# The modulation product with w_ada as the stationary operand

## The reference, cut to what matters

```python
def _adaln(cond, w, b):
    return jax.nn.silu(cond) @ w + b        # w: (1024, 6144), b: (6144,)
mod_ctx = _adaln(c_ctx[None], w_ada[l], b_ada[l])
mod_lat = _adaln(c, w_ada[l], b_ada[l])
...
shift1, scale1, gate1, shift2, scale2, gate2 = jnp.split(mod[:, None, :], N_MOD, axis=-1)
m, s_fin = _mixer(x * (1 + scale1) + shift1, lp, s0)
x = _layer_norm(DEEPNORM_ALPHA * x + gate1 * m, ...)
f = ffn(x * (1 + scale2) + shift2)
x = _layer_norm(DEEPNORM_ALPHA * x + gate2 * f, ...)
```

## Time and profile before

| | us |
|---|---|
| median of 3 runs | 2322.9 (2321.09 to 2323.04) |
| profiled execution, its time | 2311.55 |
| profiled execution, span of its core | 2309.8 |
| TensorE products busy | 2015.3 (87%) |
| TensorE loads of the stationary operand busy | 1704.7 (74%) |
| VectorE busy | 1136.7 (49%) |
| ScalarE busy | 757.7 (33%) |
| mean granted TensorE clock | 0.917 of 2.4 GHz |

### The profile page before, as it was taken

How to read it: one execution, slowest core, us unless ns; L and a number is a source line. 1 busy time by engine, 2 the same in 40 slices (tenths; PEclk the granted TensorE clock), 3 DMA queues, 4 the chain that set the end, 5 groups by cost and what they waited for, 6 DMA issues and landing times.

```text
span 2309.8 us, 30916 instructions
## 1 busy us (share of the span) xinstructions
PE 2015.3 (87%) x13189; PEld 1704.7 (74%) x13189; DVE 1136.7 (49%) x1458; ACT 757.7 (33%) x918; POOL 106.6 (5%) x161
## 2 busy tenths in 40 slices
PE   6789989986779997888988867789999999999996
PEld 2766656664669986666766646688989989899895
DVE  1645443435665546445434456644545445454454
ACT  1332222223234434222222331333433334344332
POOL 3011001000020000101001000000000000000000
PEclk9889998897989998699898979799999999999998
DMA  8403332242155553122222321435555555556552
GB/s 270 148 25 111 111 111 91 92 137 84 37 162 187 189 188 104 57 74 84 64 93 92 122 62 51 132 108 193 166 190 174 174 193 172 176 171 191 179 168 82
DMA packets 247417, 301.27 MB, mean 130 GB/s; under 512 B 8427, under 2 KB 224080, under 8 KB 247152
## 3 DMA queue, kind: packets, MB, share of 16 engines
q1 hardware_dynamic: 240112, 286.28, 38.9%
q0 software_dynamic: 4192, 11.28, 1.6%
q10 hardware_dynamic: 2976, 1.73, 0.3%
HBM read 297.69 MB, written 1.57 MB: 130 GB/s over the span
## 4 chain that ended last, share of the span: by engine, by line
PE 77%; DVE 13%; ACT 5%; issue 4%; DMA 1%; ACTq 0%; DVEq 0%; SPq 0%
PE PS L662 13%; PE PS L663 12%; PE PS L664 12%; PE PS L705 6%; PE PS L975 5%; PE PS L976 5%; PE PS L977 5%; PE PS L830 2%; DVE WL L1363 2%; ACT WH L1086 2%; PE PS L780 2%; PE PS L827 2%; PE PS L848 1%; DVE WL L1372 1%; DMA WRING<-in_w_ada 1%
## 5 line engine op out<-in xcount | busy, mean ns | idle before, releaser
L662 PE MATMUL PS<-HTH,WH 128*128 128x256 f32 x2448 | 724.0, 296 | 90.4 <-DVE WL L1372 38.0
L1363 DVE TENSOR_TENSOR WL<-WRING,WH 128x2048 fp32r<-128x2048 f32 (+1 forms) x213 | 460.3, 2162 | 529.9 <-ACT WH L1086 528.0
L663 PE MATMUL PS<-HTL,WH 128*128 128x256 f32 x2448 | 706.8, 289 | 0.0
L664 PE MATMUL PS<-HTH,WL 128*128 128x256 f32 x2448 | 706.2, 288 | 0.0
L1086 ACT ACTIVATE WH<-WRING 128x2048 fp32r<-128x2048 f32 (+1 forms) x213 | 385.8, 1811 | 686.0 <-PE PS L664 438.9
L662 PEld LDWEIGHTS PS<-HTH,WH 128*128 128x128 f32 x2448 | 480.9, 196 | 112.1 <-issue 77.9
L663 PEld LDWEIGHTS PS<-HTL,WH 128*128 128x128 f32 x2448 | 482.2, 197 | 0.7
L664 PEld LDWEIGHTS PS<-HTH,WL 128*128 128x128 f32 x2448 | 481.4, 197 | 0.0
L705 PE MATMUL PS<-WRING,CONDT 128*2 128x256 f32 x768 | 198.4, 392 | 6.7 <-DMA WRING<-in_w_ada 5.6
L975 PE MATMUL PS<-WH,AH 128*128 128x512 f32 x440 | 171.9, 391 | 13.6 <-DVE WL L1363 13.6
L977 PE MATMUL PS<-WL,AH 128*128 128x512 f32 x440 | 171.3, 389 | 0.0
(11 more groups left out here) (318 smaller groups left out, 2175.3 us busy)
## 6 DMA issues: line engine op xcount, KB each, us to landing
WRING<-in_exp_w_in SPq DMA_DIRECT2D x80, 1024.0 KB, 5.4
WRING<-in_w_ada SPq DMA_DIRECT2D x48, 1024.0 KB, 5.3
WRING<-in_w_in SPq DMA_DIRECT2D x42, 1024.0 KB, 5.6
WRING<-in_exp_w_out SPq DMA_DIRECT2D x40, 1024.0 KB, 5.0
WRING<-in_ffn_w_in SPq DMA_DIRECT2D x22, 1024.0 KB, 5.1
WRING<-in_ffn_w_out SPq DMA_DIRECT2D x11, 1024.0 KB, 5.0
WRING<-in_w_o SPq DMA_DIRECT2D x8, 1024.0 KB, 5.0
WRING<-in_exp_w_in SPq DMA_DIRECT2D x16, 512.0 KB, 3.8
```

What stands on the lines that cost most here:

```text
L662: mm(out, h[:, kb, c], hi[:, kb, :], start=kb == 0, stop=False)
L663: mm(out, h[:, kb, c], lo[:, kb, :], start=False, stop=False)
L664: last = mm(out, s[:, kb, c], hi[:, kb, :], start=False, stop=kb == k - 1)
L1363: tt(WL[:, m % 2, 0:k * w], WRING[:, n % RING, 0:k * w], WH[:, m % 2, 0:k * w].bitcast(F32), ALU.subtract)\
```

## The change

The operands of the modulation product change places. The weights become the stationary operand, 128 x 128 at a time, and the two conditions the moving one, 2 columns. A tile of 256 outputs then takes 16 calls (2 halves x 8 blocks) in place of 8, and its result comes out in the column layout at once, 128 partitions x 4 numbers in PSUM. `turn` and `line` are gone with the buffer `ADAR` they used, and so is `CONDS`, the split copy of the conditions. VectorE's `col` waits for the product itself. At the head, the product of tile j is no longer broken in two by the transposes of tile j-1. In the fill, `col` is due 2 scan steps after the last piece of its tile (before: `line` 1, `turn` 3, `col` 5).

```diff
-        sched.append(("ada", 0, j, 0, 2))
-        sched += [("turn", 0, j - 1), ("col", 0, j - 1)] if j else [("bias",)]
-        sched += [("ada", 0, j, 1, 2), ("row", 0, j)]
-    sched += [("turn", 0, ADA_HEAD - 1), ("col", 0, ADA_HEAD - 1), ("consts",), ("params", 0), ("barrier",)]
+        sched += [("ada", 0, j, 0, 1), ("row", 0, j)]
+        sched += [] if j else [("bias",)]
+        sched.append(("col", 0, j))
+    sched += [("consts",), ("params", 0), ("barrier",)]
...
-                after = [(1, ("line", m, i)), (3, ("turn", m, i)), (5, ("col", m, i))]
+                after = [(2, ("col", m, i))]
...
-                for kb in range(KB * part // parts, KB * (part + 1) // parts):
...
-                        last = mm(PS[0:2, bank_of[n], 0:256], CONDT[:, kb::8], w[:, kb, :], start=kb == 0, stop=kb == KB - 1)
+                w = tile_view(WRING, n % RING, n)
+                work = [(b, kb) for b in range(2) for kb in range(KB)]
+                for b, kb in work[len(work) * part // parts:len(work) * (part + 1) // parts]:
+                    last = mm(PS[:, bank_of[n], 2 * b:2 * b + 2], w[:, kb, b * P:(b + 1) * P], CONDT[:, kb::8],
+                              start=kb == 0, stop=kb == KB - 1)
...
-            def turn(l, j):
-                pe.wait_ge(ev("ada_row"), l * ADA + j + 1)
...
-                    last = pe.transpose(PS[:, bank_of[n], 256 + r * b:256 + r * b + r], ADAR[0:r, j % 2, b * P:(b + 1) * P],
...
-                fn(CONDS[:, :, 0:2], CONDT[:, :].rearrange("p (g k) -> p k g", g=G), ACT.Copy).then_inc(ev("cond_hi"), 1)
...
             def row(l, j):
                 make_hi(number["ada", l, j, 0] + 2)
-                line(l, j)
-
-            def line(l, j):
-                act.wait_ge(tile_done, n + 1)
...
-                fn(ADAR[0:r, j % 2, :], PS[0:r, bank_of[n], 0:256], ACT.Copy).then_inc(ev("ada_row"), 1)
...
-                dve.wait_ge(ev("cond_hi"), 1)
-                steps(tt(CONDS[:, :, 2:4], ...))
...
             def col(l, j):
-                dve.wait_ge(ev("ada_turn"), l * ADA + j + 1)
+                dve.wait_ge(tile_done, n + 1)
...
-                    tt(MODT[:, l, c, :], PS[:, bank_of[n], 256:260].rearrange("p (b c) -> p b c", c=2), bias, ALU.add)\
-                        .then_inc(dve_read, 1)
+                tt(MODT[:, l, c, :], PS[:, bank_of[n], 0:4].rearrange("p (b c) -> p b c", c=2), bias, ALU.add)\
+                    .then_inc(dve_read, 1)
```

More of the change, by code:

```diff
@@ L284, in build @@
         CONDT = sb("CONDT", [P, 16])
-        CONDS = sb("CONDS", [P, KB, 4], F32R)
-        ADAR = sb("ADAR", [4, 2, 256])
         A2 = sb("A2", [P, DR])
@@ L693, in ada @@
                     bank_free(n)
[L694 to L697, removed]
-                for kb in range(KB * part // parts, KB * (part + 1) // parts):
[L699 to L704, removed]
-                        last = mm(PS[0:2, bank_of[n], 0:256], CONDT[:, kb::8], w[:, kb, :], start=kb == 0, stop=kb == KB - 1)
+                w = tile_view(WRING, n % RING, n)
[3 more added lines that the diff above has]
+                              start=kb == 0, stop=kb == KB - 1)
                 if part == parts - 1:
                     last.then_inc(tile_done, 1)
-            def turn(l, j):
-                n = number["ada", l, j, 0]
-                pe.wait_ge(ev("ada_row"), l * ADA + j + 1)
-                r = 4 if split(n) else 2
-                for b in range(2):
-                    last = pe.transpose(PS[:, bank_of[n], 256 + r * b:256 + r * b + r], ADAR[0:r, j % 2, b * P:(b + 1) * P],
-                                        IDENT[0:r, 0:r])
-                last.then_inc(ev("ada_turn"), 1)
             def ht(l, w, g):
@@ L1063, in _ @@
                     product(number["in", a[0], a[1], 0], HTH, HTL, a[2], a[3])
-                elif what in ("gates", "resid", "z", "affine", "later", "row", "line", "mix", "split", "col", "keys", "values"):
+                elif what in ("gates", "resid", "z", "affine", "later", "row", "mix", "split", "col", "keys", "values"):
                     pass
                 else:
-                    {"cond": cond, "bias": bias, "consts": consts, "params": params, "ada": ada, "key_norms": key_norms, "turn": turn, "ht": ht, "wprep": wprep, "scan": scan,
+                    {"cond": cond, "bias": bias, "consts": consts, "params": params, "ada": ada, "key_norms": key_norms, "ht": ht, "wprep": wprep, "scan": scan,
                      "gn": gn, "sines": sines, "ht_done": ht_done, "filter": filt, "conv": conv, "merge": merge, "o": out_proj, "router": router}[what](*a)
@@ L1113, in cond @@
                 act.sem_inc(ev("cond_silu"), 1)
-                fn(CONDS[:, :, 0:2], CONDT[:, :].rearrange("p (g k) -> p k g", g=G), ACT.Copy).then_inc(ev("cond_hi"), 1)
             def row(l, j):
                 make_hi(number["ada", l, j, 0] + 2)
-                line(l, j)
-            def line(l, j):
-                n = number["ada", l, j, 0]
-                act.wait_ge(tile_done, n + 1)
-                if l * ADA + j >= 2:
-                    act.wait_ge(ev("ada_turn"), l * ADA + j - 1)
-                r = 4 if split(n) else 2
-                fn(ADAR[0:r, j % 2, :], PS[0:r, bank_of[n], 0:256], ACT.Copy).then_inc(ev("ada_row"), 1)
             def mod_columns(l, w):
@@ L1335, in _ @@
                     act.wait_ge(dve_stage, k_bar)
-                elif what in ("bias", "keys", "values", "consts", "params", "part", "ada", "turn", "col", "affine"):
+                elif what in ("bias", "keys", "values", "consts", "params", "part", "ada", "col", "affine"):
                     pass
@@ L1342, in _ @@
                 else:
-                    {"cond": cond, "row": row, "line": line, "mix": mix, "split": split_tile, "ht": ht, "ht_done": ht_done, "key_norms": key_norms, "wprep": wprep,
+                    {"cond": cond, "row": row, "mix": mix, "split": split_tile, "ht": ht, "ht_done": ht_done, "key_norms": key_norms, "wprep": wprep,
                      "scan": scan, "gn": gn, "sines": sines, "filter": filt, "conv": conv, "merge": merge,
@@ L1374, in bias @@
             def bias():
-                dve.wait_ge(ev("cond_hi"), 1)
-                steps(tt(CONDS[:, :, 2:4], CONDT[:, :].rearrange("p (g k) -> p k g", g=G), CONDS[:, :, 0:2].bitcast(F32),
-                         ALU.subtract))
                 dve.wait_ge(ev("start_ps"), 2)
@@ L1857, in _ @@
                     make_lo(number["ada", a[0], a[1], 0] + 2)
-                elif what in ("cond", "o", "part", "ada", "turn", "z", "line"):
+                elif what in ("cond", "o", "part", "ada", "z"):
                     pass
```

## The result

The changed kernel takes 2452.8 us (median of 4 runs, 2451.1 to 2463.9) against 2322.0 for the kernel before: a ratio of 1.0577, 95% interval 1.0543 to 1.0612. It is 131 us slower; the forecast was 165, with a range from 2390 to 2570 us. The profiled execution has a span of 2451.8 us against 2309.8, 142 us more; that of the kernel before was a short one (2311.55 us against the median of 2322.0).

What follows compares the result with a forecast made beforehand. TensorE, busy 87% of the span, was taken to bound the kernel. Its clock falling to half was to add 15 us in the head and 150 in the scans, +165: 2477 us profiled, 2488 median; range 2390 to 2570.

Steps and rivals of the forecast that it cites:

- The draw of the product itself: Modulation product: old and new cost about the same per tile at either clock, without the transposes.
- The first rival: Head and scans: weight loads hold the clock up, so the kernel is faster, 2315 us; chance 0.08.
- The third rival: Scans: the clock falls but waits on VectorE and ScalarE swallow it, 2350 to 2390 us; chance 0.10.
- the fourth: Scan stages: the clock falls and never comes back within a stage, about 2855 us; chance 0.04.
- The price of a tile: New product: 32 instructions at 0.112 us (full clock) or 0.213 (half), so 3.58 or 6.82 us a tile.
- The head: Head at half clock throughout: tile 6 ends at 62.5 instead of 47.4 us, +15 us.
- The scans: Modulation phases of both scan stages mostly at half clock: +150 us after deductions.
- 302 - 28 - 78 - 38: Scan phases: doubled busy time, less time already at half, each phase's start before the clock falls, and swallowed waits.
- the 40 pairs of transposes, 0.21 each: 8: Scans: removing 40 transpose pairs at 0.21 us each saves 8 us.
- the bound of 2.6 us: Scan phases: low bound for the time until the clock comes down, 51 us over the 22 phases.
- The wait on VectorE's split: Scans: 38.0 us of waits, mostly at phase ends, counted with 38 us idle; half of the 76 taken off.
- 4 us a phase: Scans: time at full clock before the clock falls in each of 22 phases, 78 us taken off.

Runs made afterwards that it cites:

- the 128-column kernel: Changed kernel with each condition streamed 64 times, 128 moving columns: 2297.8 us, ratio 0.9907; with the two removed buffers still allocated 2282.5 us, ratio 0.9843.
- equal addresses: The two removed buffers stay allocated, so later buffers keep their old addresses: changed kernel 2456.3 us, ratio 1.0600; with 128 streamed columns 2282.5 us.
- the kernel without the pairs: Old product in the changed schedule, without row copies and transposes, removed buffers still allocated, values not the reference's: 2297.3 us, ratio 0.9903 to the kernel before.
- the one with late column operations: Old product without row copies and transposes, column operation due 5 scan steps after its tile instead of 2: 2297.9 us, ratio 0.9899.
- with 64: Changed kernel with old addresses and each condition streamed 32 times, 64 moving columns: 2332.3 us, ratio 1.0060 to the kernel before.
- the head-only one: Kernel before with the new product in the 8 tiles of the head alone: 2332.0 us, ratio 1.0062.

## Why the prediction was right, and where its sizes were off

**The sign and the mechanism** were right. The draw of the product itself, the half clock and the two places are each shown: with the streaming given back under the same loads, the clock, the pace and the time come back. The first rival (loads hold the clock, 2315 us) is refuted by the head of the kernel after: 0.214 us an instruction for 41 us. The Trainium skill, TensorE: Matmul & The Clock Gate, Part 1, says that activity releases the throttled clock and that the monitor goes by how busy the engine has been. Read plainly, with back-to-back loads counted as busy, that is this rival, and the head does not agree with it. The third rival (the waits swallow it) fell too: 17 us of idle time were swallowed. So did the fourth: the clock came back between the phases, to 1.00 from 322.4 to 339.6 us for one.

**The price of a tile** was right: 0.214 at half, 0.112 at full, for the two-column product for which no row stood. The Trainium skill, TensorE: Matmul & The Clock Gate, section LDWEIGHTS, gives a load's nanoseconds as its columns over 1.2, with no word on the clock; for 128 columns that is, as an estimate, 0.107 us. The trace is near it at the full clock (0.112) and at twice it at half (0.214).

**The head** was right to 0.3 us: tile 6 at 62.8 (62.5 forecast), the stage +15.3 (15).

**The scans** were forecast at +150 and measured at +114 in the profiled execution. Set against the 128-column kernel, which removes the same things at the old clock, the forecast's parts come apart. What the clock costs: 2456.3 - 2282.5 = 174 us with equal addresses, where the sum had 15 + 158 (302 - 28 - 78 - 38) = 173. What the change removes: 36 us, where it had 8. With equal addresses the measured +137 is 174 - 36, rounded, where the forecast's +165 is 173 - 8: the whole difference is in what the change removes. That 174 meets 173 so closely is luck, as the paragraph on the 158 us below shows.

So the term that was mis-sized is "the 40 pairs of transposes, 0.21 each: 8". They measured 22 us. The 0.21 was the distance from a transpose to the next product at the head, where that product has the same two-column stationary operand. In the scans a pair stands between products of another shape. TensorE's timeline (loads and products) around one, in the kernel before:

```profile
188.67 0.20 PEld L715 LDWEIGHTS PS<-IDENT,ADAR 2*128 2x128 f32 x2
188.67 0.28 PE L715 MATMUL PS<-IDENT,ADAR 2*128 2x2 f32 x2
...
188.88 0.38 PE L662 MATMUL PS<-HTH,WH 128*128 128x256 f32 x1
```

The product in front of the pair is followed by it after a median of 0.206 us instead of 0.112, and then come 0.084 and 0.126: 0.30 us for 40 pairs are 12 us at most. The other 10 of the 22 us are not accounted for by products' distances; the scan stages of the kernel without the pairs had 21 us less of half clock than those of the kernel before, but the one with late column operations had as much as before and was as fast, so one profile each does not settle it.

The other 15 of the 36 us, by which the 128-column product beats the old one, was no term at all; the prediction called the product a draw, and inside a piece it is (3.58 against 3.45 us a tile, even 5 us dearer for the 40). It is at the ends of the pieces. Before, a piece of four instructions at the full clock, and with 128 columns one of eight:

```profile
289.64 0.44 PE L867 MATMUL PS<-IDENT,BKE 128*128 128x128 f32 x2
290.01 1.03 PE L705 MATMUL PS<-WRING,CONDT 128*2 128x256 f32 x4
290.97 0.33 PE L827 MATMUL PS<-YS,FM 128*128 128x128 f32 x1
```

```profile
286.27 1.06 PE L698 MATMUL PS<-CONDT,WRING 128*128 128x128 f32 x8
287.08 0.64 PE L812 MATMUL PS<-YS,FM 128*128 128x128 f32 x4
```

0.96 us from start to next start against 0.81, for the same work. The second is a favourable place: the medians over all such pieces at the full clock, 109 and 108 of them, are 0.956 and 0.915 us. The old piece's last product is followed after a median of 0.309 us instead of the 0.216 inside it, 0.093 more. The first one starts some 0.205 behind a product that otherwise takes 0.112, but not everywhere: behind products with 64 rows or columns of stationary operand the distance is the usual one (0.306 or 0.152). Both scans together have 138 changes in each direction. In the kernel without row copies and transposes those at the full clock add 11.6 us behind the pieces and 9.8 in front of them; in the 128-column kernel they take off 2.8. That is 24 us; less the 5 us by which the product is dearer it would be 19, where 15 were measured. This rests on distances in the traces; no run of its own shows it.

**Within the 158 us** some guesses were off and cancelled, which is luck. One reading was wrong: the clock was not down at 20.0 us; that row gives 1.00 for 17.4 to 20.0, and the trace has the fall at 20.4, so the bound of 2.6 us should have been 3.0. Idle time swallowed was 17 us, not 38. The wait on VectorE's split did not go: in the kernel after, the idle time before L660 is 84.7 us against 90.4 before L662, under other releasers' names. And of the modulation's 768 and 512 instructions, 272 and 222 started at the full clock, 35% and 43%, where 4 us a phase is 23% and 30% of the 194 and 146 us: some 40 us more at the full clock than I had taken off. The first error is 21 us too low, the second 40 too high, and the forecast's 158 would have become 139; between the profiled executions of the two-column and the 128-column kernel with equal addresses the scans differ by 85 + 64 = 149. The other 10 us are not assigned.

**Not foreseen** were the 10 us behind the second scan, from shifted addresses.

## What to carry to other kernels

Before turning a product so that its small operand moves, price two things: the loads, which set the pace however few columns stream (0.112 us an instruction here for 32-bit 128 x 128 at the full clock, with 2 as with 128 columns), and what the streaming did for the clock. If the loads set the pace, streaming the small operand many times over by a stride of zero costs no pace up to those 128 columns, and kept the clock here: 128 columns instead of 2 turned 6% slower into 1.6% faster. Small products wedged between others cost their neighbours' overlap as well as themselves; measure them in their place.

## What the runs showed of the hardware that was not expected

- TensorE at 100% busy in both rows for 41 us kept the pace of 1.2 GHz with two streamed columns (0.214 us an instruction), and with 64 (0.215); with 128 the granted clock was at 1.00 from 35.5 us on.
- With two streamed columns the clock also fell in the scans with next to no idle time in front (0.04 us or less in 7): 20 of 48 falls. With 64 and 128 columns, and in the kernel before, none of 45, 50 and 46 falls came with less than 0.80.
- The distance between products grows by 0.093 us where the stationary operand changes from 128 x 2 to another shape (0.309 instead of 0.216), and by as much from 128 x 128 to 128 x 2 (0.205 instead of 0.112); from one with 64 rows or columns to 128 x 2 it does not grow.
- A shift of all later SBUF buffers by 2176 bytes changed the pace of a three-pass wide product at 2.4 GHz from 118.3 to 120.0 ns, and putting it back restored it: 10 us in 990.
- The same scan takes different times: 443, 442 and 459 us for the first one with two streamed columns, and 395, 404 and 404 for the second, with the same instructions in them on TensorE. With the old product the first one took 370 us in the kernel before and 377 in the head-only one.
